# A value projection over all head groups at once, TensorE's loops written out, and VectorE's order in each down projection

## The reference, cut to what matters

```
h = x + 0.5 * swiglu_1(rmsnorm(x))            # 1024 -> 2816 -> 1024
u = rmsnorm(h)
cq, ckv, kr, dq, dk, dv, gl = split(u @ w_in) # dq, dk, dv: 3 groups x 4 heads x 64 = 768 columns each
A = latent attention(cq, ckv, kr)             # 8 heads
B = dilated attention(dq, dk, dv)             # windows 128, 512, 2048 with dilation 1, 4, 16
h = h + (sigmoid(gA) * (A @ w_o_mla) + sigmoid(gB) * (B @ w_o_dil)) @ w_out
h = h + 0.5 * swiglu_2(rmsnorm(h))
swiglu(x) = (silu(x @ w_gate) * (x @ w_up)) @ w_down
```

## Time and profile before

| what | value |
|---|---|
| median of 3 runs | 2853.5 us (2848.46 to 2859.66) |
| the profiled execution, its own time | 2862.61 us |
| its span | 2860.8 us |
| mean granted TensorE clock | 0.962 |
| TensorE matmuls busy | 2661.5 us, 93%, 16466 of them |
| TensorE weight loads busy | 2539.4 us, 89% |
| VectorE, ScalarE, GpSimd busy | 1096.7, 540.4, 921.6 us |

### The profile page before, as it was taken

One profiled execution on the slowest core, in us unless ns is written; L12 is line 12 of the kernel. 1 busy time (PEld: TensorE's weight loads), 2 busy tenths in 40 slices (PEclk: granted clock), 3 DMA queues, 4 the chain that ended last, 5 costly groups with the idle time before them and its releaser, 6 DMA issues.

```text
span 2860.8 us, 42488 instructions
## 1 busy us (share of the span) xinstructions
PE 2661.5 (93%) x16466; PEld 2539.4 (89%) x16466; DVE 1096.7 (38%) x1890; ACT 540.4 (19%) x1240; POOL 921.6 (32%) x468
## 2 busy tenths in 40 slices
PE   4999999999989999998899888979899999999997
PEld 4999999999979999998777766879899999999996
DVE  7232223232384643001555635375532222222226
ACT  4100000000033420113333323311220000000002
POOL 5433333333344331331000212134343333333333
PEclk9999999999999999999999898689999999999998
DMA  4121212121212331421221106254111211111111
GB/s 150 65 93 60 91 60 92 59 92 58 93 58 80 130 119 51 166 92 59 61 65 29 52 1 241 69 184 162 71 54 62 107 46 51 45 44 44 44 44 60
DMA packets 87381, 229.03 MB, mean 80 GB/s; under 512 B 8937, under 2 KB 50450, under 8 KB 86130
## 3 DMA queue, kind: packets, MB, share of 16 engines
q1 hardware_dynamic: 79082, 208.38, 21.3%
q10 hardware_dynamic: 8168, 18.70, 1.7%
HBM read 196.65 MB, written 74.39 MB: 95 GB/s over the span
## 4 chain that ended last, share of the span: by engine, by line
PE 83%; DVE 9%; issue 4%; DMA 2%; ACT 1%; POOL 1%; DVEq 0%; SPq 0%; ACTq 0%; POOLq 0%
PE ps L715 22%; PE ps L716 22%; PE ps L717 22%; PE ps L948 2%; PE ps L924 2%; PE ps L1124 1%; PE ps L841 1%; PE ps L843 1%; PE ps L842 1%; DVE xn L1553 1%; PE ps L1028 1%; DVE u_lo L406 1%; DVE rstd L1541 1%; PE ps L937 1%; POOL u_lo L406 1%
## 5 line engine op out<-in xcount | busy, mean ns | idle before, releaser
L715 PE MATMUL ps<-u_hi,w_hi 128*128 128x352 f32 (+1 forms) x2880 | 934.8, 325 | 39.8 <-DVE u_lo L406 17.4
L716 PE MATMUL ps<-u_lo,w_hi 128*128 128x352 f32 (+1 forms) x2880 | 926.6, 322 | 0.0
L717 PE MATMUL ps<-u_hi,w_lo 128*128 128x352 f32 (+1 forms) x2880 | 924.4, 321 | 0.0
L633 POOL TENSOR_TENSOR w_hi<-raw,zero 128x1024 fp32r<-128x1024 f32 x186 | 354.8, 1908 | 1405.6 <-PE ps L715 1153.1
L715 PEld LDWEIGHTS ps<-u_hi,w_hi 128*128 128x128 f32 x2880 | 546.9, 190 | 53.9 <-issue 23.5
L716 PEld LDWEIGHTS ps<-u_lo,w_hi 128*128 128x128 f32 x2880 | 547.4, 190 | 0.4 <-issue 0.2
L717 PEld LDWEIGHTS ps<-u_hi,w_lo 128*128 128x128 f32 x2880 | 546.7, 190 | 0.0
L636 POOL TENSOR_TENSOR w_lo<-raw,w_hi 128x1024 fp32r<-128x1024 f32 x186 | 454.2, 2442 | 14.6
L715 PE MATMUL ps<-h_hi,w_hi 128*128 128x352 f32 (+1 forms) x1056 | 342.8, 325 | 30.3 <-DVE x L1600 30.2
L1593 DVE TENSOR_TENSOR h<-ps,silu 128x352 f32<-128x352 f32 x132 | 68.2, 516 | 772.1 <-PE ps L717 766.9
L1600 DVE SCALAR_TENSOR_TENSOR x<-ps,x 128x352 f32<-128x352 f32 (+1 forms) x528 | 269.9, 514 | 209.4 <-PE ps L717 209.4
(11 more groups left out here) (265 smaller groups left out, 2999.2 us busy)
## 6 DMA issues: line engine op xcount, KB each, us to landing
raw<-in_wstream SPq DMA_DIRECT2D x186, 512.0 KB, 3.3
out_win_out<-in_cache_win SPq DMA_DIRECT2D x23, 1424.0 KB
latn<-in_cache_mla SPq DMA_DIRECT2D x128, 80.0 KB, 1.9
scratch_gates<-stage ACTq DMA_DIRECT2D x16, 516.0 KB, 2.7
out_win_out<-in_cache_win SPq DMA_DIRECT2D x7, 1168.0 KB
kv_d<-in_cache_win SPq DMA_DIRECT2D x24, 256.0 KB, 9.3
sgt<-scratch_gates SPq DMA_DIRECT2D x16, 352.0 KB, 3.9
scratch_x_mid<-x SPq DMA_DIRECT2D x1, 4128.0 KB, 15.0
```

The lines of the kernel that those rows point to most:

```text
L633: nc.gpsimd.tensor_tensor(w_hi[:, s], raw[:, s % RAW], zero[:].to_broadcast([P, UW]), ALU.add).then_inc(w_hi_done, 1)
L715: a = mm(out, wh, xh, start=start, stop=False)
L716: mm(out, wh, xl, start=False, stop=False)
L717: return a, mm(out, wl, xh, start=False, stop=stop)
```

## The change

The values are computed once for 128 neighbouring tokens and all 768 columns: 24 matmuls of 512 columns (groups 0 and 1) in banks 6 and 7, and 24 of 256 (group 2) in banks 4 and 5. The weights of the wide part take four ring slots, those of the narrow part two places in x (`wv_hi`, `wv_lo`). For that x has been stored before, at the end of the first feed-forward. Values are stored in natural token order (`v_nat`) and read back with the group's stride. The small norm matmuls move behind value tiles 3 and 5. TensorE's loops over pairs, gates and head pairs are Python loops, so their instructions are written out. On VectorE, `hidden` for the last tile of a pair takes a call between the product and the low part, which evicts the first block of the down projection.

```diff
@@ -165,7 +165,9 @@
         stage = at(82560, "stage", [P, 3, TOK])
-        v_stage = at(103296, "v_stage", [P, 2, 256])
+        v_stage = at(94944, "v_stage", [P, 2, NG * 256])
+        wv_hi = at(123872, "wv_hi", [P, 2, UW], F32R)
+        wv_lo = at(132064, "wv_lo", [P, 2, UW], F32R)
         swapped = at(105344, "swapped", [P, 2, TW])
@@ -490,18 +494,20 @@
             N2, N1 = (GROUPS[2][0] - 1) // ROWS2, (GROUPS[1][0] - 1) // ROWS1
-            with sp.Fori(0, N2) as i:
-                for k in range(4):
-                    sp.wait_ge(split_done, 4 * i + k + 1)
-                    load_unit(4 * i + (k + RAW), k % RAW)
-                shift_window(2, i * ROWS2, ROWS2)
+            N2A = (U_PROJ + 4) // 4
+            for part in ((0, N2A), (N2A, N2)):
+                with sp.Fori(*part) as i:
+                    for k in range(4):
+                        sp.wait_ge(split_done, 4 * i + k + 1)
+                        load_unit(4 * i + (k + RAW), k % RAW)
+                    shift_window(2, i * ROWS2, ROWS2)
+                if part[0] == 0:
+                    sp.wait_ge(down_evac, 2 + 24 * NPAIR)
+                    sp.dma_start(io["x_mid"], x[:].rearrange("p m t -> p (m t)")).then_inc(x_kept, 16)
             for n in range(4 * N2 + RAW, U_MIX):
...
                 load_unit(n, n % RAW)
-                if n == 4 * N2 + RAW + 1:
-                    sp.wait_ge(down_evac, 2 + 24 * NPAIR)
-                    sp.dma_start(io["x_mid"], x[:].rearrange("p m t -> p (m t)")).then_inc(x_kept, 16)
 
@@ -528,7 +534,9 @@
                 sp.dma_start(k_g[g % 2][:], io["k_T"][g].rearrange("c p t -> p c t")).then_inc(g_landed[g % 2], 16)
-                sp.dma_start(v_g[g % 2][:], io["v_sub"][g].rearrange("(n p) c -> p n c", p=P)
+                s = STRIDE[g]
+                sp.dma_start(v_g[g % 2][:].rearrange("p (r b) c -> p r b c", r=s),
+                             io["v_nat"][:, g * 256:(g + 1) * 256].rearrange("(b p r) c -> p r b c", p=P, r=s)
                              ).then_inc(g_landed[g % 2], 16)
@@ -670,7 +678,16 @@
             split_straight(U_PROJ + 4, U_PROJ + 6)
-            split_units(U_PROJ + 6, U_MIX)
+            split_units(U_PROJ + 6, U_V - 2)
+            split_straight(U_V - 2, U_V + 3)
+            pool.wait_ge(x_kept, 16)
+            for n in (U_V + 3, U_V + 4):
+                split_unit(n, n % RING, 16 * (n // RAW + 1), None, (wv_hi[:, n - U_V - 3], wv_lo[:, n - U_V - 3]))
+            n = U_V + 5
+            split_unit(n, n % RING, 16 * (n // RAW + 1), U_V, (w_hi[:, V_SLOT[3]], w_lo[:, V_SLOT[3]]))
+            split_units(U_GATE, U_MIX)
+            assert U_GATE % RING == 0 and (U_V - 2) % RING == 0
             assert (U_PROJ + 2) % RING == 0 and U_MIX % RING == 0 and U_FFN2 % RING == 0
@@ -775,7 +792,7 @@
                 gate_up(f0 + 1, 1, n0 + 2, 2, 2)
-                with pe.Fori(0, (NPAIR - 1) // 2) as i:
+                for i in range((NPAIR - 1) // 2):
                     for half in range(2):
@@ -823,41 +840,71 @@
 
-            for g in range(NG):
-                n = U_V + 2 * g
-                s = n % RING
-                pe.wait_ge(split_done, n + 2)
-                for i in range(9):
-                    j = 9 * g + i
-                    if j >= 2:
-                        pe.wait_ge(v_evac, j - 1)
-                    cols = group_tile(g, i) if i < 8 else slice(TOK - P, TOK)
-                    out = ps[:, 6 + j % 2, 0:256]
+            def mm3_tokens(out, k, cols, wh, wl, start, stop):
+                a = mm(out, u_hi[:, k, cols], wh, start=start, stop=False)
+                mm(out, u_lo[:, k, cols], wh, start=False, stop=False)
+                return a, mm(out, u_hi[:, k, cols], wl, start=False, stop=stop)
+            for i in range(9):
+                cols = slice(i * P, i * P + P) if i < 8 else slice(TOK - P, TOK)
+                out01, out2 = ps[:, 6 + i % 2, :], ps[:, 4 + i % 2, 0:256]
+                def both(k0, k1):
+                    for k in range(k0, k1):
+                        if i == 0 and k % 2 == 0:
+                            pe.wait_ge(split_done, U_V + (k // 2 + 1 if k < 6 else 6))
+                        part = slice((k % 2) * 512, (k % 2) * 512 + 512)
+                        a, b = mm3_tokens(out01, k, cols, w_hi[:, V_SLOT[k // 2], part], w_lo[:, V_SLOT[k // 2], part],
+                                          k == 0, k == KD - 1)
+                        if i == 0 and k == 0:
+                            a.then_inc(unit_used, 1)
+                def third():
+                    if i == 0:
+                        pe.wait_ge(split_done, U_V + 5)
                     for k in range(KD):
-                        part = (s + k // 4) % RING
-                        wh = w_hi[:, part, (k % 4) * 256:(k % 4 + 1) * 256]
-                        wl = w_lo[:, part, (k % 4) * 256:(k % 4 + 1) * 256]
-                        a = mm(out, u_hi[:, k, cols], wh, start=k == 0, stop=False)
-                        mm(out, u_lo[:, k, cols], wh, start=False, stop=False)
-                        b = mm(out, u_hi[:, k, cols], wl, start=False, stop=k == KD - 1)
-                        if i == 0 and k == 0:
-                            a.then_inc(unit_used, 1 if g == 0 else 2)
-                    b.then_inc(v_ready, 1)
-                if g == 1:
+                        part = slice((k % 4) * 256, (k % 4) * 256 + 256)
+                        a, b = mm3_tokens(out2, k, cols, wv_hi[:, k // 4, part], wv_lo[:, k // 4, part],
+                                          k == 0, k == KD - 1)
+                        if i == 8 and k == 0:
+                            a.then_inc(unit_used, 4)
+                    return b
+                if i < 2:
+                    pe.wait_ge(dve_read, n_dve_read(15, i + 1))
+                else:
+                    pe.wait_ge(v_evac, i - 1)
+                if i == 0:
+                    both(0, 6)
+                    third()
+                    pe.wait_ge(split_done, U_V + 6)
+                    for k in range(6, KD):
+                        part = slice((k % 2) * 512, (k % 2) * 512 + 512)
+                        _, last = mm3_tokens(out01, k, cols, w_hi[:, V_SLOT[3], part], w_lo[:, V_SLOT[3], part],
+                                             False, k == KD - 1)
+                else:
+                    both(0, KD)
+                    last = third()
+                last.then_inc(v_ready, 1)
+                if i == 3:
 
                     pe.wait_ge(small_sq, 3)
-                    pe.wait_ge(dve_read, n_dve_read(15, 2))
                     for t in range(NT):
...
                            ).then_inc(small_ss, 1)
-                    for t in range(NT):
-                        mm(ps[:, 3 + t, 0:TILES[t][1]], ones[:], stage[:, 2, tile(t)], start=True, stop=True
+                if i in (3, 5):
+                    for t in range(1) if i == 3 else range(1, NT):
+                        if t > 0:
+                            pe.wait_ge(small_std, t)
+                        mm(ps[:, (3, 0, 1)[t], 0:TILES[t][1]], ones[:], stage[:, 2, tile(t)], start=True, stop=True
                            ).then_inc(small_ss, 1)
...
             pe.wait_ge(rope_add, 4 * 12)
-            pe.wait_ge(small_std, 3)
+            pe.wait_ge(small_std, 6)
             for c in range(4 * NG):
@@ -878,7 +925,7 @@
             pe.wait_ge(c_ready, 2)
-            with pe.Fori(0, 4) as i:
+            for i in range(4):
                 pe.wait_ge(pw_split, i + 1)
@@ -1343,36 +1390,40 @@
             store_roped(N_CHUNK - 1)
-            def store_v(j):
-                g, i = divmod(j, 9)
-                act.wait_ge(v_evac, j + 1)
+            def store_v(i):
+                act.wait_ge(v_evac, i + 1)
                 if i < 8:
-                    act.dma_start(io["v_sub"][g, i * P:(i + 1) * P], v_stage[:, j % 2]).then_inc(v_stored[j % 2], 16)
-                else:
-                    src = v_stage[120:128, j % 2]
+                    act.dma_start(io["v_nat"][i * P:(i + 1) * P], v_stage[:, i % 2]).then_inc(v_stored[i % 2], 16)
+                    return
+                for g in range(NG):
+                    src = v_stage[120:128, i % 2, g * 256:(g + 1) * 256]
                     act.dma_start(io["v_rows"].rearrange("(b h) (g e) -> b g h e", h=GH, g=NG)[:, g],
-                                  src.rearrange("b (h e) -> b h e", h=GH)).then_inc(v_stored[j % 2], 16)
+                                  src.rearrange("b (h e) -> b h e", h=GH)).then_inc(v_stored[i % 2], 16)
                     act.dma_start(win_out[g][:, GROUPS[g][0] - 1, 1].rearrange("b h e -> b (h e)"), src
-                                  ).then_inc(v_stored[j % 2], 16)
-            for j in range(9):
@@ -1582,7 +1633,7 @@
 
-            def hidden(f, c, par):
+            def hidden(f, c, par, between=None):
                 for t in range(NT):
@@ -1591,6 +1642,8 @@
```

(41 more changed lines are left out.)

38 lines of the change are left out of this document (22 added, 16 removed).

## The result

The kernel after took 2779.93 us (median of 4 runs, 2774.21 to 2784.94); the kernel before, timed beside it, took 2853.84 (4 runs, 2848.46 to 2859.66). The ratio is 0.974, 95% interval 0.9713 to 0.9767: 74 us less, between 66 and 82. The forecast was 2767, 87 less, with a range of 2753 to 2789.

What follows compares the result with a forecast made beforehand. TensorE was taken as the bound, holding 83% of the chain of waits. Gains of 46.6 + 0 + 22.1 + 18.0 = 86.7 us take the median from 2853.5 to 2767, range 2753 to 2789.

Steps and rivals of the forecast that it cites:

- Part 4: Down projections: evicting block 0 before the lower part gains 0.90 us at each of 20, 18.0 us.
- rival C: Down projections: GpSimd gets the port first, so the new order costs 34 us instead of gaining 18; 2819, 5%.
- Part 3: TensorE's loops: written-out feed-forward bodies have no issue wait at turns, 22.1 us gained; gate and attention loops 0.
- 17.4 us of the first feed-forward: First feed-forward: excess of its four loop turns over 4 x 138.56 us, expected to go when written out.
- The 4.7 of the second feed-forward: Second feed-forward: one turn, with the fifth issue wait, is 4.7 us longer; expected to go when written out.
- Rival B: Feed-forward loops: the turn isn't the cause, the waits return at packet borders, loops gain 0; 2789, 7%.
- Rival A: Written-out TensorE code: instructions arrive late, 166 us lost against 87 gained; 2933, 3%.
- Part 1: Value projection: tiles of neighbouring tokens, all 768 columns, save 47.7 us, less 0.4 and 0.7: 46.6 gained.
- the end: End of the value projection: the last tile leaves 768 columns to copy instead of 256, costing 0.7 us.
- VectorE beside a busy GpSimd: Start of the value projection: GpSimd's unbroken splits may delay the eviction of a reused bank; 0.4 us lost.
- Part 2: x store moved to the end of the first feed-forward: 0, with up to 3 us lost if it delays a load.

Runs made afterwards that it cites:

- e9: Kernel after with two down-projection evictions instead of one ahead of the lower part on VectorE; 2810.41 us, ratio 0.9835.
- e2: Kernel before with only TensorE's two feed-forward loops written out; 2837.02 us, ratio 0.9939.
- e1: Kernel before with only VectorE's order at the down projections changed; 2832.05 us, ratio 0.9917.
- e3: Kernel before with the second and third group's values computed on neighbouring instead of strided tokens; 2811.69 us, ratio 0.9849.
- e4: Kernel after with TensorE's loops and VectorE's order put back, leaving the value projection and x store; 2832.54 us, ratio 0.9916.
- e12: Kernel before with 128 empty TensorE instructions ahead of the first feed-forward, none ahead of the second; one run, 2886.82 us.
- e6: Kernel after with GpSimd held before the fourth to sixth value unit until VectorE has read the last rope tile; 2785.44 us, ratio 0.9747.
- e7: Kernel after with the two narrow value units first in the stream and split sooner; 2772.64 us, ratio 0.9709.
- e11: Kernel after with TensorE's gate and attention loops as loops again, feed-forwards still written out; 2781.32 us, ratio 0.9739.
- e8: Kernel after with GpSimd released for its next split at block 2 instead of block 0 of each down projection; 2771.64 us, ratio 0.9698.
- e5: Kernel before with 12 empty TensorE instructions ahead of the first feed-forward and 244 ahead of the second; 2878.29 us, ratio 1.0078.

## Why the prediction was right, and by how much it was off

**Part 4, VectorE's order: right, in size too.** 1.31 of stall became 0.41, 0.90 a down projection, as forecast; 20 of them are 18 us. That the lower part keeps its end, 0.36 behind GpSimd's, held in every trace where a split is running (0.35 to 0.39 behind, in all but two places of each). The margin is narrow. In the kernel after, the lower part starts 0.69 before the split's first half ends, in e9 0.20 after the second half has begun, and there rival C's price (forecast 1.7 a down projection) is paid: 1.52. The Trainium skill, SBUF — State Buffer, section SBUF: two separate sides, speaks of an exclusive lock held for a whole instruction; these traces agree, with 0.36 between the two ends whether VectorE comes early or late.

**Part 3, the loops: the mechanism right for the first feed-forward, the term for the second unsure.** The 17.4 us of the first feed-forward came (e2: 17.6; four turns from 142.90 to 136.77, of which 1.80 is part 4). The 4.7 of the second feed-forward was real in the one execution that I read: its second turn fetched 9 packets. The profiles of e1 and e3, with the same order and number of instructions on TensorE, have neither the packets nor the wait. A profile is one execution, and I carried a wait of it into the median. How much of it the median holds isn't shown, since the intervals of e1 and e2 allow both. It also means that the position isn't all that decides: the same code at the same place fetched its body once in one execution and not at all in two others. Rival B (the waits come back at packet borders) is refuted by both profiles with straight bodies. Rival A too: packets went from 106 to 128 in all, and no feed-forward waits for one.
What I had not seen is that the parts aren't independent. The value projection changes the length of the code ahead of the second feed-forward, and in that position its loop waits at each turn (e4). Beside parts 1 and 2, the written-out loops are thus worth the eight waits, not four or five: 17.4 + 17.6 = 35 us. The forecast held for the whole only because the loops went in the same change, and that was luck: it had not seen the link. Alone, parts 1 and 2 would have been misjudged by half: 22 instead of the 41 that the value stage gains.
The Trainium skill, Runtime: NRT & Kernel Launch, section Instruction fetch mechanics, says that a taken branch to a page outside the window stalls on a fetch. Eight of eight turns do so in e4 and e12, which agrees; in e1 only four of eight do, and the second feed-forward's turns have no packet. What decides between the two no run here shows in full.

**Part 1, the values: right in its cause, 5.6 us too much.** The pace is as worked out (8.43 us a tile against 8.46, 233 ns a wide matmul), e3 shows the stride as the cause, and the end costs 0.2 instead of the 0.7 forecast. The step that failed is "VectorE beside a busy GpSimd. Bounds 0 and 1.5 us; I take 0.4." It measured 4.0, and 2.4 more followed: 12 matmuls stepping at 0.43 instead of 0.234, at a granted clock of 0.50, because TensorE had idled. The row for it was there (2.62 us for one product), but I let one such product count. A rope tile has two or three of them, they follow one another, and each sits out a split. e6 and e7 show the cause by taking it away in two ways.

**Part 2, the x store: 0 held**, as far as the waits tell: none of TensorE's at that place names a DMA. It was not run by itself. Of the written-out gate and attention loops, 0 was forecast and e11 finds none.

**The sum.** Between the two profiled executions 86.7 were forecast and 77.7 measured. Nearly all of the 9.0 between is part 1 (5.6) and small losses in other stages (0.5, 1.7 and 1.1 in the table). Between the medians it was 74 (66 to 82). Were the wait of 4.7 not in the median before, 86.7 - 4.7 - 5.6 = 76.4 would be left, and the other 2 us would lie inside the spread of the merge stage; but that is argued and not shown.

## What to carry to other kernels

Look for one shape of matmul at two paces in the same kernel: a stationary operand read with a stride of 4 or 8 elements halves the pace (about 234 against 118 ns at 256 columns), and the reordering can go into a DMA, which no wait of TensorE names here. Where VectorE works on inputs that are both in SBUF, time GpSimd's release by it: one line (e8) moved a signal two blocks and gave 8 us, while one eviction too many ahead of it (e9) cost 30. A hardware loop with a body as long as the feed-forward's (864 matmuls and their weight loads) is fragile, since an edit ahead of it can turn its waits on or off (e4, e12); loops of a third of that length cost nothing here (e11). And a wait seen once in one profile isn't yet part of the median.

## What the runs showed of the hardware that I had not expected

- Whether the second feed-forward's loop body of 864 matmuls, with a weight load each, is fetched again depends on where it begins: 0 packets and no wait (later turns of the kernel before, all turns in e1, e3 and e5), or 9 packets and 2.5 to 2.9 us at each turn (e4, e12), for the same instructions. The first feed-forward's was fetched again wherever it began. Behind such a wait the next ten or so matmuls step slower, 0.29 instead of 0.16, at a granted clock of 0.56 (e4, 2214.45 to 2218.20), which makes 4.4 us of 2.7.
- An instruction of 8 columns with both inputs in SBUF takes 2.37 us (kernel after) instead of 0.15 (e6) when GpSimd is inside an operation: that it is short doesn't help it.
- An instruction of TensorE that only raises a semaphore takes 150 ns (e5).
- After 4 us of idling the granted clock was 0.50 for 4.9 us of matmuls that follow without a gap, and 0.98 after that: a wait of 4.0 us cost 6.4.
